# RWKV's modulation slots: none in its end, twelve in its preparation, and another order there

## The chip, the cores and the metric

The kernel runs on one core of a Trainium2 chip. The metric is device time in microseconds, the median of the runs shown. TensorE multiplies, VectorE, ScalarE and GpSimd work elementwise, and SyncE asks for the transfers of weights; the five run side by side and meet at semaphores. A stage of the kernel ends for all engines together.

## What is computed

Two blocks of a network on 256 latent and 256 context tokens of width 1024, in float32. The first block has two layers, and each is steered by a modulation, computed from the condition vectors `c` and `c_ctx`:

```python
m_l = (jax.nn.silu(c) @ mod_w + mod_b)[:, None, :]
m_c = jax.nn.silu(c_ctx) @ mod_w + mod_b
sh1_l, sc1_l, g1_l, sh2_l, sc2_l, g2_l = jnp.split(m_l, 6, axis=-1)
...
def _ada(x, g, shift, scale):
    return rmsnorm(x, g) * (1.0 + scale) + shift
```

`mod_w` is 1024 x 6144 in each layer, so both are 48 MB to be read for two rows of output. The mixer of layer 0 is half attention, half an RWKV scan over the tokens, forwards and backwards. Ahead of the scan stands this preparation:

```python
a = jax.nn.sigmoid(a0 + ad @ a2)
tw = jnp.tanh(wd)
wl = -jax.nn.softplus(-(w0 + tw @ w2)) - 0.5      # decay: exp(-exp(wl))
kk = hd(k * k_k)
kk = kk / jnp.maximum(jnp.sqrt(jnp.sum(kk * kk, axis=-1, keepdims=True)), 1e-12)
k = k * (1.0 + (a - 1.0) * k_a)
g = jax.nn.sigmoid(gd) @ g2
```

## The kernel before

The program is one stage after the other, called from `program` in the order of the network. Feature rows lie on the 128 partitions, the 512 tokens along the free dimension; a width of 512 is four tiles, `t` = 0 to 3. All weights come through `RING`, four places of 1 MB.

**Modulation slots.** The 48 MB of `mod_w` are cut into 48 slots of 1 MB, 256 columns each (class `Modulation`, L402). Slot n uses ring place n mod 4. Stages that leave ring and engines some room host a range of slots, in order. A slot is four steps: SyncE's `fetch` (L429); TensorE's `add` (L434), 8 matmuls into one half of PSUM bank 7, once the slot before it is folded; ScalarE's `copy` (L447) of the sums to SBUF, which waits for the sums and for the fold before; and TensorE's `fold` (L453), two narrow matmuls that turn the copy into columns of the other half of bank 7. There is one place for the sums and one for their copy, so slots can't overlap: the sums of a slot come after the fold of the one before. At the end of the stage VectorE's `bias` (L460) adds `mod_b` to all columns of the stage's range. The first stage hosts slots 0 to 7, the attention 8 to 29, its norm 30, then RWKV's preparation 31 to 38, its back-decay stage 39 to 43, its end 44 to 47. The chunk stages between them host none: their matrices lie in the ring. The last gains (`gain`, L470) are computed in RWKV's end, and the first MLP uses them.

**The preparation** (`rwkv_prepare_stage`, L2682). On TensorE: *rates* are the products `ad @ a2`, on array rows 64 to 127, *decays* the products `tanh(wd) @ w2_f`, on rows 0 to 63; both take 512 tokens per tile. The order is rates 0 to 2, decays 0 to 2, rate 3, decay 3; then the four norm sums (L2734, `kk * kk` over a head), each once its square and a rate's sigmoid are done, since they share PSUM banks; then sixteen transposes of v (L2743); then all eight slots. On ScalarE: Tanh, four squares, the gate's Sigmoid, then sigmoids of rates (L2760) and decays (L2762) in turn; `inverse_roots` (L2528) with a load of the table for logarithm and exponential, four logarithms, which wait for VectorE's floors of the norms, and four exponentials; three exponentials of 2048 columns (L2768 to L2771) and two short ones; then four times a slot's copy and a copy of transposed tokens (L2637), and then the four copies that are left. On VectorE: sixteen scans of the decays (L2655), four floors (L2799), the centring of the decays (L2665 to L2678), then kk and the factors with GpSimd's products between them, four products of 2048 columns, and `bias`. On SyncE: the fetches of slots 35 to 38, each when the slot four before it is summed.

**RWKV's end** (`rwkv_finish_stage`, L3117). It normalizes y and gates it; VectorE's last step is the gated product of tile 3 (L3203). SyncE fetches slots 44 to 47 at the start, and then the four parts of the output weights, each when its place's slot is summed. TensorE's slots follow its last gate product; the bias and three gains come last on VectorE. The stage behind it is the first MLP (`first_mlp_stage`, L642): ScalarE copies a rounded half of a weight tile (L522), VectorE subtracts it from the whole (L529), TensorE multiplies.

Of the kernel before, what the change touches and what calls it, by code (L numbers as in the profile page):

```python
# [30 lines left out]
ACT = mybir.ActivationFunctionType  # L31
# [9 lines left out]
NCH = TOK // CH  # L41
HID = 4096
FF = 2816
SLOTS = 4
# [2637 lines left out]
def rwkv_prepare_stage(net, mod, first_slot, last_slot):  # L2682


    nc, mem = net.nc, RwkvMemory(net)
# [6 lines left out]
    with Stage(net, "rwkv_prepare") as st:  # L2692
# [16 lines left out]
        def _(pe):  # L2709
# [10 lines left out]
            rates(0)  # L2720
            rates(1)
            rates(2)
            pe.wait_ge(tanh_ready, 1)
            for t in range(3):
                decays(t)
            rates(3)
            decays(3)
            for t in range(4):
                pe.wait_ge(squared, t + 1)
                if t < 3:  # L2730
                    pe.wait_ge(a_ready, t + 2)
                else:
                    pe.wait_ge(gated, 3)
                nc.tensor.matmul(norm_in[t], net.const(C_BLK), square[:, t, :], start=True, stop=True).then_inc(normed, 1)  # L2734
            for c in range(NCH):
                if c < 2:
                    pe.wait_ge(gated, c + 1)
                elif c == 2:
                    pe.wait_ge(gated, 4)
                else:  # L2740
                    pe.wait_ge(floor_ready, 1)
                for t in range(4):
                    last = nc.tensor.transpose(turned_in[c][:, P * t:P * t + P], mem.v_pairs[:, t, c, :],  # L2743
                                               net.const(C_IDENT))
                last.then_inc(turned, 1)
            for n in range(first_slot, last_slot + 1):
                mod.add(pe, n, first_slot)
# [3 lines left out]
        def _(act):  # L2751
            link = Chain(act, act_own)
            net.log_exp_loaded = False
            act.activation(net.PT[0:64, lora, :], net.PT[0:64, lora, :], ACT.Tanh).then_inc(tanh_ready, 1)
            for t in range(4):
                act.activation(square[:, t, :], k[t], ACT.Square, scale=net.par("l0_k_k", t)).then_inc(squared, 1)
            act.activation(net.PT[:, gate, :], net.PT[:, gate, :], ACT.Sigmoid)
            for t in range(4):
                act.wait_ge(a_summed, t + 1)
                act.activation(b[t], a_in[t], ACT.Sigmoid, bias=net.par("l0_a0", t)).then_inc(a_ready, 1)  # L2760
                act.wait_ge(summed, t + 1)
                act.activation(rows(mem.sig[:, t]), decay_in[t], ACT.Sigmoid,  # L2762
                               bias=net.par("l0_w0_f", t)).then_inc(gated, 1)
            inverse_roots(net, act, link, root_ready, [(floor_ready, t + 1, norm[:, t, :], norm[:, t, :], 1.0, 0.0)
                                                       for t in range(4)])
            kr = mem.kr.rearrange("p t c n m -> p (t c) n m")
            act.wait_ge(cum_ready, 1)
# [7 lines left out]
            for c in range(NCH):  # L2775
                mod.copy(act, first_slot + c)
                act.wait_ge(turned, c + 1)
                copy_tokens(act, mem.vtok, net.ps[(4, 5, 0, 2)[c]], c)
            for n in range(first_slot + NCH, last_slot + 1):
                mod.copy(act, n)  # L2780
# [335 lines left out]

def rwkv_finish_stage(net, mod, first_slot, last_slot, following):  # L3117

# [8 lines left out]
    with Stage(net, "rwkv_finish") as st:  # L3127
# [7 lines left out]
        @st.sync  # L3135
        def _(sp):
            for n in range(first_slot, last_slot + 1):
                mod.fetch(sp, n)
            taken = [n % SLOTS for n in range(first_slot, last_slot + 1)]
            for s in sorted(range(following.first()), key=lambda s: s in taken):  # L3140
                if s in taken:
                    sp.wait_ge(mod.summed, first_slot + taken.index(s) + 1)
                net.fetch(sp, following, 0, s)
# [7 lines left out]
        def _(pe):  # L3151
# [10 lines left out]
            for t in range(4):  # L3162
                pe.wait_ge(root_ready, t + 1)
                nc.tensor.matmul(gate[t], net.G2[:, P * t:P * t + P], net.PT[:, 25, :], start=True,
                                 stop=True).then_inc(gate_ready, 1)
            for n in range(first_slot, last_slot + 1):
                mod.add(pe, n, first_slot)
            mod.fold(pe, last_slot, first_slot)

        @st.scalar  # L3170
        def _(act):
# [4 lines left out]
            for t in range(4):  # L3176
# [3 lines left out]
                                                       for t in range(4)])  # L3180
            for n in range(first_slot, last_slot + 1):
                mod.copy(act, n)

        @st.vector
        def _(dve):
# [9 lines left out]
            for t in range(4):  # L3195
# [7 lines left out]
                nc.vector.tensor_tensor(y[:, t, :], y[:, t, :], gate[t], ALU.mult)  # L3203
            link(mod.bias(dve, (first_slot, last_slot), first_slot, last_slot))
            for layer, half_of in ((0, 1), (1, 0), (1, 1)):
# [641 lines left out]
def program(nc, ins, out):  # L3847
    with ExitStack() as ctx:
# [25 lines left out]
                                            for h, o in enumerate(heads)], TOK, 1e-5, mod=mod, slot=30)  # L3874
        rwkv_prepare_stage(net, mod, 31, 38)
        rwkv_chunks_stage(net, 0)
        rwkv_back_decay_stage(net, mod, 39, 43)
        rwkv_chunks_stage(net, 1)
        rwkv_finish_stage(net, mod, 44, 47, w_out[0])
        mod.spent(mod.FIRST, mod.ALL - 1)  # L3880
# [25 lines left out]
```

## Time and profile before

| | us |
|---|---|
| median of 3 runs | 2114.11 |
| lowest, highest | 2112.74, 2120.26 |
| profiled execution, device time | 2122.14 |
| its span | 2120.3 |
| preparation, 304.1 to 353.0 | 48.9 |
| RWKV's end, 611.4 to 635.8 | 24.4 |

The profile shows one execution. Times in its rows count from the start of the span. A row of a timeline has the start, the time from the first start to the last end, the engine, the line, the tiles written and read, the count, and, in brackets, how long the engine was idle before and what released it. A float32 matmul is two instructions (a wide and a narrow one of 16 per slot in a slot's sums). PE is TensorE, DVE VectorE, ACT ScalarE; the granted clock is given in parts of 2.4 GHz, so 0.50 is 1.2 GHz.

### The profile page before, as it was taken

To read this page: it belongs to the slowest core of one execution; us is meant where nothing else is said; L and a number is where in the kernel's file an instruction comes from. 1 tells how busy PE (TensorE), PEld (TensorE's weight loads), DVE (VectorE), ACT (ScalarE), POOL (GpSimd) and SP (SyncE) were. 2 spreads that over 40 slices of the span, in tenths; PEclk is the share of its full clock that TensorE was granted. 3 is DMA by queue.
4 is the path that set the end of the run, shared out by engine and by line. 5 is a ranking of instruction groups with operands and counts; after the bars stand their busy time and mean duration, and the time that the engine had idled before them with its cause. 6 is when DMAs were issued, how large, how long until landed. Compare 5 with 4: busy or idle time off the path is not lost. (4 is left out here: it accounts for less than half of the span.)

```text
span 2120.3 us, 41961 instructions
## 1 busy us (share of the span) xinstructions
PE 1929.4 (91%) x18072; PEld 1674.4 (79%) x18072; DVE 1203.5 (57%) x2057; ACT 838.2 (40%) x1532; POOL 295.7 (14%) x351
## 2 busy tenths in 40 slices
PE   5998887778789999999999879999989998989997
PEld 3886545767757888888978779999769998869997
DVE  3322757455445742453465858856567756577753
ACT  3321564324223421222344545544464445365432
POOL 2000304402304000002200420112021001121001
PEclk8999886997999999999999999999999999999998
DMA  9232762011042322332231055554325545324543
GB/s 323 85 100 74 255 207 81 4 48 56 4 135 85 100 97 82 100 100 92 88 119 40 21 166 162 192 181 158 100 80 166 192 152 186 100 76 154 190 154 105
DMA packets 249004, 255.04 MB, mean 120 GB/s; under 512 B 6914, under 2 KB 247187, under 8 KB 248691
## 3 DMA queue, kind: packets, MB, share of 16 engines
q1 hardware_dynamic: 247344, 251.19, 36.8%
q8 instruction: 143, 2.34, 0.5%
q0 software_dynamic: 864, 0.98, 0.2%
q14 instruction: 43, 0.34, 0.1%
q10 hardware_dynamic: 610, 0.18, 0.0%
HBM read 251.28 MB, written 1.05 MB: 119 GB/s over the span
## 5 line engine op out<-in xcount | busy, mean ns | idle before, releaser
L529 DVE TENSOR_TENSOR RING_rounded<-RING,SC_rounded 128x1024 fp32r<-128x1024 f32 (+2 forms) x390 | 459.7, 1222 | 281.9 <-ACT SC_rounded L522 281.7
L549 PE MATMUL bank<-OT_rounded,SC_rounded 128*128 128x256 f32 (+1 forms) x1808 | 576.2, 319 | 27.3 <-DVE PT L1268 11.5
L550 PE MATMUL bank<-HT_rounded,SC_rounded 128*128 128x256 f32 (+1 forms) x1808 | 572.3, 317 | 0.0
L551 PE MATMUL bank<-OT_rounded,RING_rounded 128*128 128x256 f32 (+1 forms) x1808 | 570.4, 315 | 0.0
L522 ACT ACTIVATE SC_rounded<-RING 128x1024 fp32r<-128x1024 f32 (+2 forms) x390 | 372.4, 1006 | 324.4 <-DMA RING<-in_l_mlp_w 186.2
L549 PEld LDWEIGHTS bank<-OT_rounded,SC_rounded 128*128 128x128 f32 x1808 | 345.0, 191 | 56.5 <-issue 13.6
L551 PEld LDWEIGHTS bank<-OT_rounded,RING_rounded 128*128 128x128 f32 x1808 | 344.2, 190 | 25.7
L550 PEld LDWEIGHTS bank<-HT_rounded,SC_rounded 128*128 128x128 f32 x1808 | 344.6, 191 | 22.6
L549 PE MATMUL bank<-PT_rounded,SC_rounded 128*128 128x256 f32 (+1 forms) x896 | 278.5, 311 | 4.7 <-DVE RING_rounded L529 4.7
L550 PE MATMUL bank<-PT_rounded,SC_rounded 128*128 128x256 f32 (+1 forms) x896 | 277.7, 310 | 0.0
L551 PE MATMUL bank<-PT_rounded,RING_rounded 128*128 128x256 f32 (+1 forms) x896 | 276.7, 309 | 0.0
L549 PEld LDWEIGHTS bank<-PT_rounded,SC_rounded 128*128 128x128 f32 x896 | 169.1, 189 | 16.3 <-DVE RING_rounded L529 5.7
L551 PEld LDWEIGHTS bank<-PT_rounded,RING_rounded 128*128 128x128 f32 x896 | 169.2, 189 | 10.8
L550 PEld LDWEIGHTS bank<-PT_rounded,SC_rounded 128*128 128x128 f32 x896 | 169.2, 189 | 9.5
L550 PE MATMUL bank<-OT_rounded,SC_rounded 128*128 128x256 f32 (+1 forms) x336 | 102.5, 305 | 0.0
L549 PE MATMUL bank<-HT_rounded,SC_rounded 128*128 128x256 f32 (+1 forms) x272 | 85.6, 315 | 16.2 <-DVE OT_rounded L1456 7.5
L3090 DVE TENSOR_TENSOR SC<-SC,bank 128x512 f32<-128x512 f32 (+1 forms) x80 | 51.3, 684 | 71.3 <-PE bank L2984 70.8
L795 DVE SCALAR_TENSOR_TENSOR XT<-bank,MOD,XT 128x256 f32<-128x256 f32 x48 | 21.4, 480 | 116.7 <-PE bank L551 116.7
L551 PE MATMUL bank<-HT_rounded,RING_rounded 128*128 128x256 f32 (+1 forms) x272 | 84.5, 311 | 0.0
L549 PEld LDWEIGHTS bank<-HT_rounded,SC_rounded 128*128 128x128 f32 x272 | 54.0, 198 | 19.9 <-DVE RING_rounded L529 13.0
L443 PE MATMUL bank<-RING,SC 128*32 128x256 f32 x768 | 66.2, 474 | 3.7 <-DMA RING<-in_l_mod_w 3.7
L456 PEld LDWEIGHTS bank<-CONST,SC 128*128 128x128 f32 x192 | 32.3, 238 | 46.1 <-ACT SC L451 45.0
(536 smaller groups left out, 2793.1 us busy)
## 6 DMA issues: line engine op xcount, KB each, us to landing
RING<-in_l_mlp_w SPq DMA_DIRECT2D x64, 1024.0 KB, 5.2
RING<-in_l_mod_w SPq DMA_DIRECT2D x48, 1024.0 KB, 6.9
RING<-in_w_ffn_in SPq DMA_DIRECT2D x44, 1024.0 KB, 5.1
RING<-in_l_w_in SPq DMA_DIRECT2D x25, 1024.0 KB, 5.3
RING<-in_w_ffn_out SPq DMA_DIRECT2D x16, 768.0 KB, 4.3
RING<-in_w_in SPq DMA_DIRECT2D x10, 1024.0 KB, 5.2
RING<-in_w_ffn_out SPq DMA_DIRECT2D x16, 640.0 KB, 3.9
RING<-in_l_w_out SPq DMA_DIRECT2D x8, 1024.0 KB, 6.2
```

The costliest lines, as they stand in the source:

```text
L443: last = self.nc.tensor.matmul(self.sums[group, :], self.c[:, kt, :], self.net.RING[:, s, SW * kt:SW * kt + SW], start=(i == 0), stop=(i = ...
L456: last = self.nc.tensor.matmul(self.columns[:, 2 * (n - first) + m, :], self.rows[:, P * m:P * m + P], self.net.const(C_FOLD, 2), start=Tr ...
L522: act.activation(net.high4(s, m)[:, 0:self.w.kts[s], :], net.ring_half(net.RING, s, m, self.w.kts[s]), ACT.Copy).then_inc(self.high_ready, 1)
L529: net.nc.vector.tensor_tensor(low, whole, net.high4(s, m)[:, 0:self.w.kts[s], :].bitcast(F32), ALU.subtract).then_inc(self.split_ready, 1)
L549: net.nc.tensor.matmul(bank[:, tokens], high, x_high, start=start, stop=False)
L550: net.nc.tensor.matmul(bank[:, tokens], high, x_low, start=False, stop=False)
L551: return net.nc.tensor.matmul(bank[:, tokens], low, x_high, start=False, stop=stop)
L795: return nc.vector.scalar_tensor_tensor(into, bank[:, tokens], net.MOD[:, gate + tile, j:j + 1], into, ALU.mult, ALU.add)
L3090: nc.vector.tensor_tensor(inv, inv, bank, ALU.subtract).then_inc(doubled, 1)
```

## The change

- RWKV's end hosts no slots. Its fetches, sums, copies, folds and `bias` go; the loads of the output weights wait for nothing; the three gains stay.
- The preparation hosts slots 31 to 42, twelve instead of eight. The back-decay stage hosts 43 to 47, five as before, in the same ring places.
- In the preparation TensorE does rate 0, all four decays, then rates 1 to 3, then the norms. The sums of the first two slots stand between the norms and the transposes, the others behind the transposes.
- On ScalarE the squares and the decays' sigmoids come in pairs (two squares, two sigmoids, two squares, two sigmoids), then the rates' sigmoids, then the gate's. The copies of the first two slots stand ahead of `inverse_roots`, the third behind it, and from the fourth on one stands behind each copy of tokens.

```diff
-            rates(1)
-            rates(2)
             pe.wait_ge(tanh_ready, 1)
-            for t in range(3):
+            for t in range(4):
                 decays(t)
-            rates(3)
-            decays(3)
+            for t in range(1, 4):
+                rates(t)
...
+            for n in range(first_slot, first_slot + 2):
+                mod.add(pe, n, first_slot)
             for c in range(NCH):
...
-            for n in range(first_slot, last_slot + 1):
+            for n in range(first_slot + 2, last_slot + 1):
                 mod.add(pe, n, first_slot)
             mod.fold(pe, last_slot, first_slot)
...
-            for t in range(4):
-                act.activation(square[:, t, :], k[t], ACT.Square, scale=net.par("l0_k_k", t)).then_inc(squared, 1)
-            act.activation(net.PT[:, gate, :], net.PT[:, gate, :], ACT.Sigmoid)
+            squares(range(2))
+            gates(range(2))
+            squares(range(2, 4))
+            gates(range(2, 4))
             for t in range(4):
                 act.wait_ge(a_summed, t + 1)
                 act.activation(b[t], a_in[t], ACT.Sigmoid, bias=net.par("l0_a0", t)).then_inc(a_ready, 1)
-                act.wait_ge(summed, t + 1)
-                act.activation(rows(mem.sig[:, t]), decay_in[t], ACT.Sigmoid,
-                               bias=net.par("l0_w0_f", t)).then_inc(gated, 1)
+            act.activation(net.PT[:, gate, :], net.PT[:, gate, :], ACT.Sigmoid)
+            for n in range(first_slot, first_slot + 2):
+                mod.copy(act, n)
             inverse_roots(net, act, link, root_ready, [(floor_ready, t + 1, norm[:, t, :], norm[:, t, :], 1.0, 0.0)
                                                        for t in range(4)])
+            mod.copy(act, first_slot + 2)
...
             for c in range(NCH):
-                mod.copy(act, first_slot + c)
                 act.wait_ge(turned, c + 1)
                 copy_tokens(act, mem.vtok, net.ps[(4, 5, 0, 2)[c]], c)
-            for n in range(first_slot + NCH, last_slot + 1):
+                mod.copy(act, first_slot + 3 + c)
+            for n in range(first_slot + 3 + NCH, last_slot + 1):
                 mod.copy(act, n)
...
-        rwkv_prepare_stage(net, mod, 31, 38)
+        rwkv_prepare_stage(net, mod, 31, 42)
         rwkv_chunks_stage(net, 0)
-        rwkv_back_decay_stage(net, mod, 39, 43)
+        rwkv_back_decay_stage(net, mod, 43, 47)
         rwkv_chunks_stage(net, 1)
-        rwkv_finish_stage(net, mod, 44, 47, w_out[0])
+        rwkv_finish_stage(net, mod, w_out[0])
```

`squares(some)` is the line of the squares for these tiles, and `gates(some)` waits for the decay product of each tile and takes its sigmoid. In RWKV's end the lines with `first_slot` and `last_slot` are gone, and SyncE's part is a loop of `net.fetch(sp, following, 0, s)` over the four places.

## Rows read from the trace of the kernel before

**Rows 1.** The head of the profile's page.
```profile
span 2120.3 us, 41961 instructions
```

**Rows 2.** Busy time by stretch; the line of columns stands first.
```profile
core 0: us, PE busy (x) PEld busy (x) DVE busy (x) ACT busy (x) POOL busy (x), PEclk, DMA share, GB/s
304.10:353.00 48.90, 37.48 (x200) 19.41 (x200) 34.64 (x42) 30.94 (x54) 15.82 (x8) 0.61 0.29 93
...
611.40:635.80 24.40, 21.70 (x112) 10.18 (x112) 14.45 (x24) 11.00 (x20) 4.97 (x4) 0.93 0.89 286
```

**Rows 3.** Timeline, ScalarE, the preparation: start, duration, instruction, idle before.
```profile
305.90 2.54 ACT L2756 ACTIVATE HT<-PT,PAR 128x512 f32<-128x512 f32 x4
308.46 1.28 ACT L2757 ACT_TABLE_LOAD   x1
...
315.03 1.28 ACT L2524 ACT_TABLE_LOAD   x1
317.49 2.42 ACT L2534 ACTIVATE OT<-OT 128x512 f32<-128x512 f32 x4 [1.18 <-DVE OT L2799]
...
322.05 1.90 ACT L2768 ACTIVATE PT<-SC 128x2048 f32<-128x2048 f32 x1
...
327.66 0.36 ACT L451 ACTIVATE SC<-bank 128x256 f32<-128x256 f32 x1
327.92 1.54 ACT L2637 ACTIVATE SC<-bank 64x256 f32<-64x256 f32 x4
...
351.30 0.38 ACT L451 ACTIVATE SC<-bank 128x256 f32<-128x256 f32 x1 [3.00 <-PE bank L443]
```

**Rows 4.** Timeline, TensorE, the preparation.
```profile
307.07 1.06 PE L2717 MATMUL bank<-PT,LORA 64*128 64x512 f32 x1
307.23 1.06 PE L2713 MATMUL bank<-PT,LORA 64*128 64x512 f32 x1
307.92 1.06 PE L2717 MATMUL bank<-PT,LORA 64*128 64x512 f32 x1
...
312.19 1.06 PE L2717 MATMUL bank<-PT,LORA 64*128 64x512 f32 x1
313.17 4.49 PE L2734 MATMUL bank<-HT,CONST 128*128 128x512 f32 x8
...
319.34 1.07 PE L443 MATMUL bank<-RING,SC 128*32 128x256 f32 x16
328.08 1.01 PE L456 MATMUL bank<-CONST,SC 128*128 128x2 f32 x4 [7.67 <-ACT SC L451]
```

**Rows 5.** Timeline, VectorE, the preparation.
```profile
324.67 0.74 DVE L2803 SCALAR_TENSOR_TENSOR HT<-PT,PAR,OT 128x512 f32<-128x512 f32 x1
...
352.79 0.19 DVE L466 TENSOR_TENSOR MOD<-bank,PAR 128x32 f32<-128x32 f32 x1 [6.41 <-PE bank L456]
```

**Rows 6.** Stretches, TensorE alone, then all engines: granted clock, DMA share, GB/s.
```profile
314.00:315.00 1.00, 1.00 (x3) 0.60 0.00 0
332.00:353.00 21.00, 17.76 (x123) 0.50 0.47 151
353.00:358.00 5.00, 4.64 (x44) 0.50 0.00 2
...
475.00:480.00 5.00, 3.62 (x28) 1.93 (x32) 4.86 (x8) 1.48 (x2) 0.00 (x0) 0.52 1.10 348
```

**Rows 7.** Timelines, RWKV's end: TensorE, then VectorE, then ScalarE.
```profile
625.62 1.07 PE L443 MATMUL bank<-RING,SC 128*32 128x256 f32 x16
...
627.73 1.07 PE L443 MATMUL bank<-RING,SC 128*32 128x256 f32 x16
...
630.72 0.69 DVE L3203 TENSOR_TENSOR OT<-OT,bank 128x512 f32<-128x512 f32 x1
...
635.40 0.35 DVE L473 SCALAR_TENSOR_TENSOR AFF<-MOD,PAR 128x16 f32<-128x16 f32 x3
...
636.09 2.00 ACT L522 ACTIVATE SC_rounded<-RING 128x1024 fp32r<-128x1024 f32 x2 [2.00 <-PEq L193]
```

More of the change, by code:

```diff
@@ L2754, in _, with squares, gates @@
             act.activation(net.PT[0:64, lora, :], net.PT[0:64, lora, :], ACT.Tanh).then_inc(tanh_ready, 1)
-            for t in range(4):
-                act.activation(square[:, t, :], k[t], ACT.Square, scale=net.par("l0_k_k", t)).then_inc(squared, 1)
-            act.activation(net.PT[:, gate, :], net.PT[:, gate, :], ACT.Sigmoid)
+            def squares(some):
+                for t in some:
+                    act.activation(square[:, t, :], k[t], ACT.Square, scale=net.par("l0_k_k", t)).then_inc(squared, 1)
+            def gates(some):
+                for t in some:
+                    act.wait_ge(summed, t + 1)
+                    act.activation(rows(mem.sig[:, t]), decay_in[t], ACT.Sigmoid,
+                                   bias=net.par("l0_w0_f", t)).then_inc(gated, 1)
+            squares(range(2))
+            gates(range(2))
+            squares(range(2, 4))
+            gates(range(2, 4))
             for t in range(4):
@@ L3114, in _, with rwkv_finish_stage @@
                     nc.vector.tensor_tensor(out, out, bank, ALU.add).then_inc(out_taken, 1)
-def rwkv_finish_stage(net, mod, first_slot, last_slot, following):
+def rwkv_finish_stage(net, mod, following):
     nc, eps = net.nc, 64e-5
@@ L3136, in _ @@
         def _(sp):
[L3137 to L3142, printed above, removed]
+            for s in range(following.first()):
                 net.fetch(sp, following, 0, s)
@@ L3165, in _ @@
                                  stop=True).then_inc(gate_ready, 1)
-            for n in range(first_slot, last_slot + 1):
-                mod.add(pe, n, first_slot)
-            mod.fold(pe, last_slot, first_slot)
         @st.scalar
@@ L3180, in _ @@
                                                        for t in range(4)])
-            for n in range(first_slot, last_slot + 1):
-                mod.copy(act, n)
         @st.vector
@@ L3203, in _ @@
                 nc.vector.tensor_tensor(y[:, t, :], y[:, t, :], gate[t], ALU.mult)
-            link(mod.bias(dve, (first_slot, last_slot), first_slot, last_slot))
             for layer, half_of in ((0, 1), (1, 0), (1, 1)):
```

## The prediction

> **What bounds the kernel now.** I read the page's head first: one core, a profiled span of 2120.3 us [rows 1]. Shares over the span say little about this change, so the next view is the table by stretch [rows 2]: the preparation takes 48.9 us at a mean granted clock of 0.61, RWKV's end 24.4 us at 0.93. The chunk stages between them and all that follows from 636.09 on the change does not touch; they can only start earlier or later. So the question is where each of the two stages ends. The reader should look at the last instruction of each engine in each.
>
> In the preparation ScalarE runs without a pause until 315, waits for VectorE's floors, does logarithms and roots from 317.49 on, from 322.05 three exponentials, and only then, at 327.66, the copy of the first hosted slot [rows 3]. TensorE had finished that slot's sums at 319.34 + 1.07 = 320.4 and stood idle for 7.7 us [rows 4]. From there the eight slots go one behind the other, copy to copy (351.30 - 327.66) / 7 = 3.38 us [rows 3], at a granted clock of 0.50, the 1.2 GHz level [rows 6]. VectorE's own work is over at 346.4, 6.4 us before its bias at 352.79, which waits for the last fold and ends the stage [rows 5]. **The preparation is bound by a serial line of slots behind ScalarE's roots and exponentials.**
>
> In RWKV's end a slot takes 2.11 us (627.73 - 625.62), since the clock is still high, and most of the line lies beside VectorE's gating, which ends at 631.41; the bias and the gains end at 635.75 [rows 7]. The first MLP's first weight copy follows at 636.09 [rows 7].
>
> **RWKV's end, without its four slots.** The bias goes, the three gains of 0.35 us together stay and can follow the gating: 631.41 + 0.35 = 631.76 against 635.75 [rows 7]. The gain is **4.0 us**, not four slots' time, because the rest was hidden. The four loads of the output weights are now asked for at the stage's start, behind no wait; the weight copy came straight after the stage change before, so they save nothing more and cost nothing (at worst 0, at best 0.3 us). TensorE ended cold before and will be idle a little longer; its cold start in the MLP is there in both.
>
> **Back-decay.** Its five slots are renumbered by four and keep their ring places. Zero.
>
> **The preparation, first part: TensorE.** A decay or a rate is two instructions of 0.85 us each at this clock (307.92 - 307.07) [rows 4]. In the kernel before, rates on rows 64 to 127 lie beside decays on rows 0 to 63: one starts at 307.23 between two decays at 307.07 and 307.92 [rows 4]. The new order puts all four decays in a row, then three rates in a row. Decays start at 306.05 after the Tanh and end at about 308.1, 309.8, 311.5 and 313.2, as late as before (the last decay instruction started at 312.19 [rows 4]). The first rate can overlap the last decay, the others can't: they end near 314.1, 315.8 and 317.5. So the first norm matmul starts at about 317.4 where it started at 313.17: **+4.2 us**.
>
> The Trainium skill, "TensorE: Matmul & The Clock Gate", section on packing small matmuls by row and column tiling, says that matmuls in different row groups run side by side while those of one group don't. The rows agree, and it speaks against this change: by a chip that paid nothing for the new order the +4.2 would be 0 and the sum 7.4; by the rule and the rows it is 11.6.
>
> The eight norm instructions took 4.49 us before [rows 4], the first ones at 0.85 and, after the clock had risen to 2.4 GHz, 1.6 us after the first norm had started (the mean grant of 314 to 315 is 0.60 [rows 6]), at 0.43. I found no row in which rates or decays alone brought the clock up, so I don't count on it before the norms. If all eight are warm they take 3.4, if all are cold 6.8; the chunks' start took over 4.6 us to warm [rows 6], the norms before 1.6, so I take five cold, 5.5, ending at **322.9** (320.9 to 324.3) where it was 317.7.
>
> **ScalarE and VectorE up to there.** Squares 0 and 1 end at 307.2, the Sigmoid table's load (1.28 us [rows 3]) at 308.5. Decay sigmoids at 0.57 us apart then wait for the decays: they end at 309.1, 310.6, 312.4 and 314.0 against 315.0 [rows 3]. So "decays first" brings the scans about 1.4 us forward, but VectorE then waits for the norms, and its gain is nothing. The rate sigmoids come at 313.9, 314.5, 315.9 and 317.6, the gate's ends at 318.8. Squares ran under Tanh's set before, between its load and Sigmoid's [rows 3]; that they also run under Sigmoid's is not shown; if not, two more loads of 1.28 come.
>
> **Two slots ahead of the roots.** The first slot's sums need the norms out of the way: 322.9 + 1.07 [rows 4] = 324.1, copy 0.36, fold and second sums to 326.2, second copy ends at 326.6, by the 2.11 us warm period of [rows 7]. ScalarE waits for both; queued behind these waits are its roots and exponentials, and behind the roots VectorE's kk chain and GpSimd's eight products. The load of the logarithm's table, hidden at 315.03 in a wait before, now stands in the open: 326.6 + 1.28 = 327.9. The logarithms started at 317.49 before [rows 3]: **+10.4 us**. All behind it on ScalarE moves with it, and the third slot's copy adds 0.36: exponentials at 332.8 against 322.05. VectorE's chain from kk, which started at 324.67 and ended at 346.4 [rows 5], starts with the first root at about 331.0 and ends near 352.7. That is not the bound.
>
> The Trainium skill, "ScalarE: Activation LUTs", section "What ACT_TABLE_LOAD costs", counts 1.38 us of drain beside each load's 1.28. The rows don't: a Sigmoid follows the load that started at 308.46 within 1.3 us [rows 3]. With the drain the sum would be 1.4 higher.
>
> **The tail.** From the exponentials' start to the first copy behind them were 327.66 - 322.05 = 5.6 us [rows 3]; then comes one block of token copies of 1.5 us [rows 3], now ahead of the slot's copy: the fourth slot is copied at 332.8 + 5.6 + 1.5 = 339.9. TensorE idles until then (its sums are done by 336), so it's cold, as it was at 327.66. Nine slots remain, eight periods of 3.38: the last copy at 367.0 where it was at 351.30, **+15.7 us**. SyncE's loads for slots five to twelve wait for the sums four slots back; the first two come at about 324 and 326, and loads don't bind: one slot in 3.38 us is less than the 348 GB/s that the queue gave elsewhere, 3.0 us a slot [rows 6]. What follows the last copy is the same.
>
> **Sum.** 10.4 (roots late) + 0.36 (third copy) + 1.5 (tokens first) + 3.38 (one more slot behind) = 15.6; less 4.0 = **+11.6 us**. On the profiled execution's own 2122.14 us (span 2120.3) that is 2133.8. The median shown is 2114.11, 8 us lower for the same program, so I carry the difference over: **2125.7 us**.
>
> **Rivals.**
> *The clock stays high in the tail.* If the spread slots keep TensorE warm, the period isn't 3.38 but 2.11 [rows 7], then bounded by loads at 3.0 us a slot for the last four, which are asked for only when a ring place is free (first at about 341.5): the last slot lands near 356, the stage ends near 358.5, +5.6, and the net is +1.5: 2115.6, not slower. It decides at the fourth slot: warm or cold when the line starts. For it: RWKV's end ran its first slots warm [rows 7], at a mean grant of 0.93 [rows 2]. Against: there they followed 14 us of dense work; and in 332 to 353 the same pattern never rose from 0.50 [rows 6].
> *The front part isn't the bound either.* Rates and decays overlap all the same or the clock rises early, so that the norms end at 317, the roots start at 322, and the tail is warm too: the last slot is bound by loads, near 352. Net about -5: 2109. Against it are the row pairs in [rows 4] and the two waits on ScalarE.
> *The reloads.* Square isn't in the Sigmoid set: two loads of 1.28 before the last decay sigmoids, the rate sigmoids and norms behind them, about +2.5: 2128.2. For it: nothing shows squares under this set. Against: they ran under Tanh's without a load of their own [rows 3].
> *The change does not do what it says:* if the three early copies were all that mattered (as much work hidden as moved), the tail would be 9 slots against 8, +3.4, and the net -0.6. This is the whole idea of the spread; it fails where ScalarE waits for TensorE ahead of the roots. Price 2113.5.
>
> **Chances.** Main case 0.78, with its own range of 2120 to 2131 (norms warm or cold 2 to 3 us, clock phases at the starts of chunks and MLP 1 to 2 us each, medians 1 to 2 us). Warm tail 0.08, spread as meant 0.04, front not bound 0.03, reloads 0.07. The range 2114 to 2132 takes in the warm tail and the reloads. What a measurement of this kernel can tell from no change is about 0.5%, 10.6 us; the forecast lies one us beyond it. Of the main case a good half is above: 0.78 x 0.58 + 0.07 x 0.9 = 0.52 slower; 0.03 faster; 0.45 within.
>
> **What would show it.** Right: the first norm matmul near 317.4; logarithms near 328; a gap on ScalarE between the gate's sigmoid and the first slot copy; fourth slot's copy near 340 and 3.38 us from copy to copy behind it; the bias near 368.5; RWKV's end 4 us shorter. Wrong: logarithms before 323 (the waits were hidden), copies 2.1 to 3.0 us apart (warm tail), extra table loads between squares and sigmoids, or VectorE's last product later than the last fold.

## The result and the profile after

The changed kernel takes 2126.59 us (median of 11 runs, 2120.08 to 2129.83), the kernel before 2116.55 us over the 11 runs beside them (2109.49 to 2120.44). The ratio is 1.0042, with a 95% interval from 1.0029 to 1.0056, which is +8.9 us (6 to 12). The forecast was +11.6 us.

Stages read off both traces, in us. The preparation is counted from ScalarE's first table load to the end of VectorE's `bias`, RWKV's end from TensorE's first matmul to the end of the last gain (the times are rounded after the differences are taken):

| stage | before | after | difference |
|---|---|---|---|
| ahead of the preparation | 304.1 | 303.4 | -0.6 |
| preparation | 48.9 | 61.6 | +12.7 |
| chunks, first | 115.9 | 115.4 | -0.5 |
| back-decay | 25.4 | 26.3 | +0.9 |
| chunks, second | 117.1 | 116.9 | -0.3 |
| RWKV's end | 24.3 | 20.2 | -4.1 |
| the rest | 1484.6 | 1481.4 | -3.2 |
| span | 2120.3 | 2125.2 | +4.9 |

The preparation and RWKV's end together give +8.6 us, +9.5 with back-decay; both lie in the interval of the timed runs. The span alone would say +4.9; the rest moved by 3 us in a part that nothing touched, so the spans of one pair of profiles don't settle a difference of this size. The changed stages can be compared one by one.

The stretches that answer to [rows 2] (columns as there):

```profile
303.40:365.10 61.70, 47.08 (x280) 24.15 (x280) 35.23 (x42) 32.56 (x58) 15.86 (x8) 0.62 0.44 142
623.60:643.90 20.30, 14.22 (x32) 5.91 (x32) 14.20 (x23) 9.46 (x16) 4.98 (x4) 0.96 0.64 207
```

TensorE's timeline of the preparation, to set beside [rows 4] (L2717 are decays, L2713 rates):

```profile
309.01 1.22 PE L2713 MATMUL bank<-PT,LORA 64*128 64x512 f32 x1
309.85 1.06 PE L2717 MATMUL bank<-PT,LORA 64*128 64x512 f32 x1
310.02 1.06 PE L2713 MATMUL bank<-PT,LORA 64*128 64x512 f32 x1
...
311.41 0.59 PE L2713 MATMUL bank<-PT,LORA 64*128 64x512 f32 x1
313.27 1.12 PE L2713 MATMUL bank<-PT,LORA 64*128 64x512 f32 x2 [1.27 <-ACT PT L2772]
314.32 5.40 PE L2732 MATMUL bank<-HT,CONST 128*128 128x512 f32 x8
319.65 1.07 PE L443 MATMUL bank<-RING,SC 128*32 128x256 f32 x16
...
329.32 1.02 PE L456 MATMUL bank<-CONST,SC 128*128 128x2 f32 x4 [3.25 <-ACT SC L451]
330.27 1.93 PE L443 MATMUL bank<-RING,SC 128*32 128x256 f32 x16
336.77 1.01 PE L456 MATMUL bank<-CONST,SC 128*128 128x2 f32 x4 [4.57 <-ACT SC L451]
```

The rates 1 and 2, issued behind all decays, run beside the last two decays: they start at 309.01, 310.02, 310.87 and 311.41 and end at 312.0. Then TensorE waits 1.27 us for ScalarE before rate 3, and the norms follow rate 3. The first norm stands 10.9 us behind the stage's start where it stood 9.1 behind it. The eight norm instructions take 5.40 us where they took 4.49. A slot's sums take 1.07 us at first and 1.93 once TensorE has waited 3.25 us for ScalarE's third copy.

ScalarE's timeline, to set beside [rows 3]:

```profile
315.01 0.62 ACT L2773 ACTIVATE PT<-PT 128x512 f32<-128x512 f32 x1
320.79 0.38 ACT L451 ACTIVATE SC<-bank 128x256 f32<-128x256 f32 x1 [5.15 <-PE bank L443]
322.90 0.38 ACT L451 ACTIVATE SC<-bank 128x256 f32<-128x256 f32 x1 [1.73 <-PE bank L443]
323.30 1.28 ACT L2524 ACT_TABLE_LOAD   x1
324.59 2.19 ACT L2534 ACTIVATE OT<-OT 128x512 f32<-128x512 f32 x4
...
336.33 0.38 ACT L451 ACTIVATE SC<-bank 128x256 f32<-128x256 f32 x1
...
363.38 0.38 ACT L451 ACTIVATE SC<-bank 128x256 f32<-128x256 f32 x1 [3.00 <-PE bank L443]
```

Here is the change in seven lines: ScalarE waits 5.15 and 1.73 us for the first two slots, the table's load stands behind them in the open, the logarithms come 21.1 us into the stage instead of 13.4, and from the fourth copy on the line runs at (363.38 - 336.33) / 8 = 3.38 us. VectorE had its products done at 349.2 and waits; the line that answers to [rows 5]:

```profile
364.86 0.21 DVE L466 TENSOR_TENSOR MOD<-bank,PAR 128x48 f32<-128x48 f32 x1 [15.64 <-PE bank L456]
```

RWKV's end on VectorE, to set beside [rows 7]: the gains follow the last gated product directly.

```profile
642.89 0.69 DVE L3206 TENSOR_TENSOR OT<-OT,bank 128x512 f32<-128x512 f32 x1
643.50 0.34 DVE L473 SCALAR_TENSOR_TENSOR AFF<-MOD,PAR 128x16 f32<-128x16 f32 x3
```

### The profile page after: what moved, and what is told of

It is laid out like the page before. It is cut to its first block and busy times, and to the rows that moved or that the text cites. A ratio compares the mean times of both kernels' runs of the same rounds, so it can differ in the third digit from the quotient of the medians.

```text
span 2125.2 us, 41960 instructions
## 1 busy us (share of the span) xinstructions
PE 1927.4 (91%) x18072; PEld 1670.5 (79%) x18072; DVE 1201.6 (57%) x2056; ACT 838.3 (39%) x1532; POOL 296.1 (14%) x351
## 5 line engine op out<-in xcount | busy, mean ns | idle before, releaser
L549 PEld LDWEIGHTS bank<-OT_rounded,SC_rounded 128*128 128x128 f32 x1808 | 345.1, 191 | 56.7 <-issue 13.5
L775 ACT ACTIVATE PT<-bank 128x512 f32<-128x512 f32 x32 | 18.9, 598 | 123.9 <-PE bank L551 123.9
```

The lines of the kernel that those rows point to most:

```text
L549: net.nc.tensor.matmul(bank[:, tokens], high, x_high, start=start, stop=False)
L775: act.activation(hidden.whole[:, 2 * q + m, :], part.bank(q, m)[:, :], ACT.Relu).then_inc(part.taken, 1)
```

## Experiments

The theory to test: the preparation ends with a serial line of slots, whose period is set by TensorE's clock, and RWKV's end gives back only what was not hidden. All runs are timed beside the kernel before, 5 to 12 times each; the ratio of a run is its time over that of the kernel before, with its 95% interval behind it. "Into the stage" counts from ScalarE's first table load of the preparation. *Warm* is a granted clock of 1.00 (2.4 GHz), *cold* one of 0.50 (1.2 GHz), and the *period* is the time from one slot's copy to the next. Stage times come from one profiled execution of each run.

### The two halves of the change, each alone

The allotment of the change with the old order of the preparation:

```diff
-        rwkv_prepare_stage(net, mod, 31, 38)
+        rwkv_prepare_stage(net, mod, 31, 42)
...
-        rwkv_finish_stage(net, mod, 44, 47, w_out[0])
+        rwkv_finish_stage(net, mod, w_out[0])
```

> The allotment of the change alone (31 to 42 in the preparation, none in RWKV's end) with the preparation's order of the kernel before. Theory (the preparation ends with the serial line of slots, 3.38 us each behind ScalarE's exponentials): first copy 24 us after the stage's first ScalarE instruction as before, eleven periods of 3.38 behind it, so the preparation is 4 x 3.38 = 13.5 us longer than before, RWKV's end 4.0 shorter, net +9.5 us, ratio 1.0045. That is about what the whole change measured, so its new order is worth nearly nothing. Rival (the new order is what costs): without it the time stays within 0.15% of before. Rival (the new order saves much): over +13 us.

The ratio is 1.0043 (1.0026 to 1.0059). The first copy comes 23.6 us into the stage and the twelfth at 60.75; the stage takes 62.45 us and RWKV's end 20.2. That is as the theory has it.

The new order with the old allotment (the change's `rwkv_prepare_stage`, the rest of the kernel before):

> The change's new order in the preparation alone, with the allotment of before (31 to 38, 39 to 43, 44 to 47). Theory: the fourth copy comes 32.9 us after the stage's first ScalarE instruction, as in the changed kernel, and four periods of 3.38 follow it instead of nine slots' eight: the preparation is 61.6 - 13.5 = 48.1 us against 48.9; VectorE's products then end near its line of slots, 46 us after the start, so they do not bind. Net -0.8 us, ratio 0.9996. Rival (the order itself costs some 9 us): ratio above 1.003.

The ratio is 0.9997 (0.9983 to 1.0012) and the stage takes 48.06 us, as expected; the last copy is at 46.4 us and VectorE's products end at 45.8. So **the +0.42% is the allotment's, and the order is worth nothing that can be measured.** Its three early copies shorten the line by three periods, 10 us, and its late logarithms (+7.7), plus a block of token copies now ahead of the fourth copy (+1.5), give nearly all of that back.

RWKV's end alone. This kernel leaves out the fetches, sums, copies and folds of slots 44 to 47 and sets their columns, the last gate, to zero, so what it computes is not the network:

```diff
-            link(mod.bias(dve, (first_slot, last_slot), first_slot, last_slot))
+            nc.vector.memset(net.MOD[:, 88:96, :], 0.0).then_inc(own, 1)
+            dve.wait_ge(own, link.n + 1)
```

> The kernel before with slots 44 to 47 left out altogether (the last eight columns of the modulation are set to zero), so RWKV's end is that of the changed kernel and nothing else is moved. Theory: most of the four slots was hidden beside VectorE's gating, so the end is 4.0 us shorter and the kernel too, ratio 0.9981. Rival (the slots cost their full 4 x 2.11 = 8.4 us, or free loads start the MLP earlier): ratio 0.996.

The ratio is 0.9957 (0.9942 to 0.9972). The trace shows that stage at 20.35 us, 3.9 shorter, and a span 3.2 us shorter; the timed runs show 9 us (6 to 12). The stage is as the theory has it, but the timed kernel gained more than its stage, which is the number of the rival, and this stays open. The profiled execution was the slowest of the five, 2118.98 us where the median is 2111.75. In it no stage holds 8 us, and the MLP's first weight copy starts 0.3 us behind the gains, as in the kernel before, so the rival's reasons don't show either. The run with the allotment alone has the same empty end, and there the stages (+13.5 and -4.1) account for the whole. What the zeros do to the time behind this stage was not tested.

### What delays the logarithms

The table's load moved ahead of the two copies, in the changed kernel:

```diff
+            load_log_exp(net, act)
             for n in range(first_slot, first_slot + 2):
                 mod.copy(act, n)
```

> The changed kernel with the load of the table for logarithm and exponential placed ahead of the first two slot copies, where ScalarE waits for TensorE anyway. Theory: the logarithms start 1.28 us earlier and all behind them, the line of slots too: the preparation 60.3 us instead of 61.6, ratio to before 1.0036 where the change has 1.0042. Rival (copies need another table, or the load is followed by a drain): no gain, or a second load in the trace.

The ratio is 1.0047 (1.0034 to 1.0060), so there is no gain, and the stage takes 62.6 us. ScalarE's timeline of this run, and TensorE's rate 3:

```profile
308.84 1.28 ACT L2524 ACT_TABLE_LOAD   x1
314.73 0.38 ACT L451 ACTIVATE SC<-bank 128x256 f32<-128x256 f32 x1 [4.61 <-PE bank L443]
316.84 0.38 ACT L451 ACTIVATE SC<-bank 128x256 f32<-128x256 f32 x1 [1.73 <-PE bank L443]
317.12 2.18 ACT L2534 ACTIVATE OT<-OT 128x512 f32<-128x512 f32 x4
```

```profile
305.52 2.07 PE L2713 MATMUL bank<-PT,LORA 64*128 64x512 f32 x2 [1.19 <-ACT PT L2772]
```

The load is hidden now: from the second copy to the logarithms it's 0.28 us instead of 1.69. But in this execution TensorE's eight norm instructions took 6.14 us instead of 5.40 and started 12.5 us into the stage instead of 10.9, at the lower clock, so the first sums came 2.4 us later and ate the 1.4. The edit isn't the cause of that: the load stands behind the sigmoids that the norms need, and the run with filler in the changed kernel, without this edit, also has its first norm at 12.5. The load is hidden as expected; that the stage gets shorter by it is not shown, and 1.3 us is less than the timed runs can tell.

Rates 1 and 2 ahead of the decays again, in the changed kernel:

```diff
             rates(0)
+            rates(1)
+            rates(2)
             pe.wait_ge(tanh_ready, 1)
             for t in range(4):
                 decays(t)
-            for t in range(1, 4):
-                rates(t)
+            rates(3)
```

> The changed kernel with rates 1 and 2 issued ahead of the decays again, so that both row groups of the array are in use together; decays 0 to 3 still ahead of rate 3. Theory (rates behind decays delay the norms): rates 1 and 2 are done 3 us earlier, but in the changed kernel TensorE stood idle 1.27 us before rate 3 for the first rate's sigmoid, which itself comes behind the decays' sigmoids on ScalarE, so the first norm moves at most 1 us forward; what may change more is the clock at the norms, granted 0.50 in the changed kernel (5.40 us for eight) and 1.00 at best (3.4 us). The stage is 0 to 3 us shorter. Rival (the issue order is what delays the norms, +4.2 us as predicted): the logarithms start over 3.5 us earlier.

The ratio is 1.0049 (1.0032 to 1.0066), and the stage takes 61.97 us. TensorE's timeline of this run:

```profile
299.62 1.06 PE L2713 MATMUL bank<-PT,LORA 64*128 64x512 f32 x1
300.19 1.06 PE L2717 MATMUL bank<-PT,LORA 64*128 64x512 f32 x1
300.47 1.06 PE L2713 MATMUL bank<-PT,LORA 64*128 64x512 f32 x1
301.04 3.14 PE L2717 MATMUL bank<-PT,LORA 64*128 64x512 f32 x6
306.19 2.07 PE L2713 MATMUL bank<-PT,LORA 64*128 64x512 f32 x2 [2.01 <-ACT PT L2773]
308.19 5.61 PE L2733 MATMUL bank<-HT,CONST 128*128 128x512 f32 x8
```

Rates 1 and 2 are done early, and TensorE only waits longer ahead of rate 3, 2.01 us for the first rate's sigmoid. The first norm starts 11.0 us into the stage, the changed kernel's 10.9, but the two are alike by two differences that cancel: the clock was up during the decays and down again behind them (1.00 in 302 to 305, 0.50 in 305.5 to 308), so rate 3 starts at 9.0 us instead of 9.8 and takes 2.07 us instead of 1.12. What tells is the wait. In the changed kernel too, rates 1 and 2 are over with the decays and rate 3 waits 1.27 us, and 1.19 in the run with the table's load ahead of the copies, which is cold up to the norms. **What delays the norms is ScalarE's order (all decay sigmoids ahead of the first rate's, whose bank rate 3 needs), not TensorE's.** No run puts the first rate's sigmoid back ahead of the decays' alone.

### What sets the period

The kernel before, with matmuls that nobody reads behind each slot's sums, so that TensorE doesn't rest:

```diff
+            def filler(count, width):
+                for _ in range(count):
+                    nc.tensor.matmul(net.ps[3][:, 0:width], net.const(C_ONES), net.CONST[:, 0:width], start=True, stop=True)
+
+            pe.wait_ge(floor_ready, 4)
             for n in range(first_slot, last_slot + 1):
                 mod.add(pe, n, first_slot)
+                filler(*((8, 512) if n == first_slot else (1, 256)))
```

The filler writes to a bank from which VectorE takes the last floors' input, hence the wait for them; the first sums start about 15.2 us into the stage, as before.

> The kernel before with products nobody reads on TensorE: eight of 512 columns behind the first slot's sums, while ScalarE is busy, and one of 256 columns behind each later slot's sums. Theory (the period of 3.38 us is that of TensorE at the lower clock): the clock stays high in the line of slots, the period falls to between 2.2 and 3.0 us (the loads' bound at 348 GB/s for 1 MB), the line ends at 24 + 7 x 2.2 to 3.0 = 39 to 45, and the stage at 44 to 46 us instead of 48.9; net -3 to -5 us, ratio 0.998. Rival (the period is set by the chain of semaphores and copies whatever the clock): period over 3.2 us, and the filler adds to it.

The ratio is 0.9970 (0.9957 to 0.9983), and the stage takes 42.45 us. The granted clock (TensorE alone, columns as in [rows 6]) and three of the copies:

```profile
319.00:327.00 8.00, 7.63 (x28) 1.00 0.41 133
327.00:343.00 16.00, 15.12 (x156) 1.00 0.61 198
```

```profile
328.94 0.38 ACT L451 ACTIVATE SC<-bank 128x256 f32<-128x256 f32 x1 [0.29 <-PE bank L443]
...
331.05 0.38 ACT L451 ACTIVATE SC<-bank 128x256 f32<-128x256 f32 x1 [0.30 <-PE bank L443]
...
333.17 0.38 ACT L451 ACTIVATE SC<-bank 128x256 f32<-128x256 f32 x1 [0.29 <-PE bank L443]
```

The clock stays at 2.4 GHz and the period is 2.11 us, with a matmul more in it than the 3.38 us one; only the last copy comes 2.8 us behind the one before it, since its load is late. The line now ends beside VectorE's products, which end the stage. So the period is set by TensorE's clock.

The changed kernel with the same, three and six wide ones behind the third and fourth slot's sums and one narrow one behind each later slot's:

> The changed kernel with products nobody reads behind the sums of slots three to twelve, three and six of 512 columns where ScalarE is busy, one of 256 columns behind each later slot. Theory (the change is slow only since its slots run at the lower clock, as the filler run on the kernel before showed for its own): fourth copy at 32.9 us after the stage's start as in the changed kernel, then a period of 2.11, or up to 3.0 where the loads bind, since eight slots are now asked for one by one: last copy at 50 to 57, the preparation 51 to 58 us instead of 61.6, ratio to before 0.998 to 1.001. Rival (the loads bind harder, as ring places come free late): period over 3.0 and the stage over 59 us.

The ratio is 1.0006 (0.9989 to 1.0023), and the stage takes 55.07 us. The fourth copy is 35.3 us into the stage (the norms were late and cold in this execution, the first at 12.5), then six copies follow 2.11 to 2.19 us apart and the last two 2.98 and 2.76. This is the warm tail that the prediction had as a rival, with a net of +1.5 us; +1.3 (-2.3 to +4.9) is measured, which agrees within a wide interval.

### Copies where ScalarE doesn't wait

The kernel before with its first copies ahead of each long exponential and behind the last:

```diff
+            mod.copy(act, first_slot)
             act.activation(kr[:, :, 1, :], flat(mem.cum), ACT.Exp, scale=-DECAY).then_inc(exped, 1)
+            mod.copy(act, first_slot + 1)
             act.activation(flat(mem.bd), flat(mem.cum), ACT.Exp, scale=DECAY).then_inc(exped, 1)
+            mod.copy(act, first_slot + 2)
             act.wait_ge(cum_ready, 2)
...
+            mod.copy(act, first_slot + 3)
             for c in range(NCH):
-                mod.copy(act, first_slot + c)
                 act.wait_ge(turned, c + 1)
                 copy_tokens(act, mem.vtok, net.ps[(4, 5, 0, 2)[c]], c)
+                mod.copy(act, first_slot + 4 + c)
```

> The kernel before, its order and its allotment, with the first four slot copies placed where ScalarE never waits for them: ahead of each of the three long exponentials and behind the last. Theory: each costs ScalarE 0.3 us and takes a period of 3.38 off the line behind it; copies 2 to 4 may follow each other at ScalarE's 2.1 us, so four slots are done by about 25 us after the stage's start and four are left: the line ends at about 24.9 + 4 x 3.38 = 38.5, which puts VectorE's products at the end, 42.3 + 1: the stage 43.5 to 44 us instead of 48.9. Net -5, ratio 0.9976. Rival (the copies delay the exponentials and these VectorE's products as much as they save): within 1 us of before.

The ratio is 0.9972 (0.9958 to 0.9986), and the stage takes 43.28 us. The sum came out as forecast, by another way: the copies were 3.4 us apart from the first on, not 2.1, since TensorE had rested 2.8 us ahead of the first copy.

```profile
320.89 0.36 ACT L451 ACTIVATE SC<-bank 128x256 f32<-128x256 f32 x1
321.15 1.90 ACT L2769 ACTIVATE PT<-SC 128x2048 f32<-128x2048 f32 x1
324.24 0.38 ACT L451 ACTIVATE SC<-bank 128x256 f32<-128x256 f32 x1 [1.20 <-PE bank L443]
...
327.62 0.38 ACT L451 ACTIVATE SC<-bank 128x256 f32<-128x256 f32 x1 [1.19 <-PE bank L443]
```

It brings the line 5.6 us forward, since the first copy comes at 18.0 instead of 23.6 us into the stage, and it costs VectorE nothing: its products end at 42.3 as before.

One slot more here and one less in RWKV's end (31 to 39, 40 to 44, 45 to 47):

> As the run with the copies among the exponentials, but nine slots in the preparation, five in back-decay and three in RWKV's end. Theory: the line of nine ends 3.4 us later, at about 42, still beside VectorE's products, so the preparation stays at 44; RWKV's end loses its one slot behind VectorE's gating, 2.7 us (the fourth slot was run at the lower clock). Net -7.5 us, ratio 0.9965. Rival (no slot is free any more): the preparation is 3.4 us longer than in the run with eight and the net no better.

The ratio is 0.9961 (0.9942 to 0.9980). The preparation takes 46.68 us, 3.4 longer than with eight slots in the run above, which is the rival's; RWKV's end takes 21.15, where the run above has 23.3. The two ratios can't be told apart. At the lower clock there's no free slot.

### Both together, and where the slots belong

Copies among the exponentials, filler in the preparation (three wide ones behind the first slot's sums, one narrow behind each later slot's) and, with four wide ones ahead of its first slot and five behind its second, in back-decay; three allotments.

> The order of the kernel before, twelve slots in the preparation and none in RWKV's end as in the change, the first four copies among the exponentials, filler in the preparation's and in back-decay's line of slots. Theory: copies from 18.0 us on at 2.11, then at the loads' 3.0 us a slot; slot five is asked for at 15.2 us, so the twelfth lands at about 15 + 5 + 7 x 3.0 = 41 to 42 and the line ends at 44, level with VectorE's products: preparation 44 to 46 us (48.9 before), RWKV's end 20.2 (24.3), back-decay 23 (25.4). Net -9 to -11 us, ratio 0.995 to 0.996. Rival (loads bind, each asked for only when a place is free): preparation over 48, net less than -6.

The ratio is 0.9953 (0.9936 to 0.9969). The preparation takes 47.27 us, back-decay 25.18 and RWKV's end 20.21. The twelfth copy comes 46.0 us into the stage: from the eighth slot on, TensorE waits for loads.

```profile
327.52 1.07 PE L443 MATMUL bank<-RING,SC 128*32 128x256 f32 x16 [0.71 <-DMA RING<-in_l_mod_w]
...
330.50 1.07 PE L443 MATMUL bank<-RING,SC 128*32 128x256 f32 x16 [0.79 <-DMA RING<-in_l_mod_w]
...
333.64 1.07 PE L443 MATMUL bank<-RING,SC 128*32 128x256 f32 x16 [0.96 <-DMA RING<-in_l_mod_w]
```

3.0 to 3.1 us a slot, as estimated from [rows 6], but the twelfth slot's sums start 44.8 us into the stage, where its landing was put at 41 to 42. In back-decay the filler didn't keep the clock up in this execution: the granted clock is 0.51 in 459 to 466.

> The same with the allotment of before (8, 5, 4): copies among the exponentials, filler in preparation and back-decay. Theory: the preparation is bound by VectorE, 42.5 us; back-decay 23; RWKV's end 24.3: net -8.5 us, ratio 0.996; the four slots taken out of RWKV's end in the run with twelve would then be worth 4.0 less what the preparation is longer. Rival (filler costs power and the clock falls elsewhere, or the rest of the kernel is slower): stages as told but the whole not.

The ratio is 0.9956 (0.9939 to 0.9973). The preparation takes 42.45 us and is ended by VectorE, back-decay takes 22.85, at a granted clock of 1.00, and RWKV's end 24.34. Timed, twelve and eight slots come out level. By the stages twelve cost 4.8 us in the preparation and give 4.1 in RWKV's end; the 2.3 us between the two back-decay stages is their clock.

> Copies among the exponentials and filler in preparation and back-decay, with ten slots in the preparation, five in back-decay, two in RWKV's end. Theory: in the run with twelve the tenth copy came 40.2 us after the stage's start, so ten slots end at 41.7, beside VectorE's work, which ends at 42.4: preparation 42.5 to 43; two slots in RWKV's end take 4.2 us behind the gate products and end beside VectorE's gating, so that stage is 20.3 to 20.6. Against before -6 (preparation), -2.4 (back-decay), -3.8 (RWKV's end): -12 us, ratio 0.9943. Rival (RWKV's end still shows a slot): that stage 22 us, and the ratio that of the runs with eight or twelve, 0.9955.

It takes 2101.29 us (median of six) against 2118.66, a ratio of **0.9917** (0.9897 to 0.9937), the fastest version of all. The preparation takes 42.47 us, back-decay 22.85 and RWKV's end 20.41. The last rows of both stages on VectorE show that neither has a wait in front of `bias`:

```profile
335.41 2.29 DVE L2826 TENSOR_TENSOR PT<-PT 128x2048 f32<-128x2048 f32 x1
337.62 0.19 DVE L466 TENSOR_TENSOR MOD<-bank,PAR 128x40 f32<-128x40 f32 x1
```

```profile
609.92 0.69 DVE L3220 TENSOR_TENSOR OT<-OT,bank 128x512 f32<-128x512 f32 x1
610.52 0.16 DVE L466 TENSOR_TENSOR MOD<-bank,PAR 128x8 f32<-128x8 f32 x1
610.72 0.35 DVE L473 SCALAR_TENSOR_TENSOR AFF<-MOD,PAR 128x16 f32<-128x16 f32 x3
```

The stages account for 6.4 + 2.6 + 3.9 = 12.9 us of the 17.6 (13 to 22). The other 4.7 are, as in the run with the empty end, not found in a stage that was changed. In the profile the two chunk stages are 1.8 and 1.3 us shorter than in the kernel before, but over all profiles these stages, which no run touches, take 113.7 to 118.8 and 115.9 to 120.8 us, so one profile doesn't show where the rest was gained.

## Why the prediction was right

**What bounds the stage** held: a serial line behind ScalarE's exponentials, at 3.38 us a slot at 1.2 GHz. The filler runs show the clock as its cause, and the run with the allotment alone shows the price, four periods.

**RWKV's end**: forecast -4.0, measured -4.1, by the step that was given (the gains directly behind the gating). The size belongs to this execution of the kernel before, whose fourth slot ran partly cold (0.59 granted in 631.5 to 635.7). In the runs with the order alone and with the copies among the exponentials the same four slots ran warm and the stage took 23.3 us, which would make the gain 3.1.

**Back-decay**: forecast 0, measured +0.9 in this profile. The run with the order alone has 25.40, the one with filler in the preparation alone 26.32. In the changed kernel this stage's eight decay instructions took 5.93 us instead of 3.67, at a mean grant of 0.61 instead of 1.00, since the clock fell 1.3 us into the stage. In the filler run it fell there too; in every run without filler in this stage in which it stayed high for 2.5 us or more the stage takes 25.4 whatever the preparation hosts, twelve slots included. So the +0.9 is the clock's in this execution, not the new numbering's.

**TensorE's first part** is the step that failed. It put the first norm 4.2 us later; it came 1.8 us later. The sentence that fails is "The first rate can overlap the last decay, the others can't". In the changed kernel rates 1 and 2 lie beside the last two decays and end at 312.0 with them, where the prediction had them end at about 314.1 and 315.8, and rate 3, the only one left over, waits for the first rate's sigmoid. So a delay is there, but by ScalarE's order and not by rates standing in a row. The prediction computed when that sigmoid would come, but by its row of rates it wouldn't have been waited for. In the two executions of this order that stay cold the first norm comes at 12.5 us, 3.4 later than before; that leaves 0.8 of the 2.4 us of error to this step.

The other 1.6 us are the clock. "I found no row in which rates or decays alone brought the clock up" was taken for a reason. In the changed kernel it did rise during the decays, at about 311, fell again at about 314.5, under the norms, and came back at about 318:

```profile
306.00:312.00 6.00, 6.00 (x12) 0.58 0.00 0
314.00:315.00 1.00, 1.00 (x2) 0.74 0.00 0
315.00:317.00 2.00, 2.00 (x4) 0.50 0.00 0
318.00:320.00 2.00, 2.00 (x12) 1.00 0.00 0
```

The run with the order alone has the same rise; the two cold ones don't, so it is not a property of the kernel. The old order shows it as well: in six of its nine profiles the clock is up about 4 us into the stage and the first norm comes at 8.2 us, in three, the kernel before among them, at 9.1. The logarithms start at 13.4 in all nine. Before, the norms had room; in the new order they have none.

The Trainium skill's rule on row groups ("TensorE: Matmul & The Clock Gate", section on packing small matmuls) agrees with the overlap in both traces. Rates and decays lie in different row groups in either order; the prediction took the order of issue to end their overlap, and it did not.

**The norms**: 5.5 forecast, 5.40 measured, cold for the first 3.4 us and then warm. That it fits so well is partly luck: four of the eight were cold where five were put, and the clock had been up before the norms began. Where it hadn't, they took 6.14 us.

**Two slots ahead of the roots**: the two waits and the load in the open stood where they were forecast, 2.5 us from the first sums' end to the second copy's end (326.6 - 324.1) where 2.6 are measured (323.3 - 320.7), and 1.3 of load. The logarithms came +7.7 instead of +10.4; the difference of 2.7 is the 2.4 us of the first norm and 0.3 of the steps behind it.

**The drain** that the Trainium skill counts with a table load ("ScalarE: Activation LUTs", section "What ACT_TABLE_LOAD costs") does not show: from the load at 323.30 to the first logarithm at 324.59 are 1.29 us.

**The tail** had all its terms right, eight periods of 3.38, the tokens' 1.5 and the third copy's 0.36; the last copy came +12.7 instead of +15.7 since its start did.

**The rivals.** The warm tail's price agrees with the run with filler in the changed kernel; it didn't come by itself. The reloads didn't come: the two later squares ran under the Sigmoid set without a load. The total of +11.6 lies inside the interval of 6 to 12 us, and the chances leaned to slower by over 0.5% (0.52) rather than within (0.45); the 2.7 us by which the logarithms came earlier than forecast, 2.4 of them the first norm's, are what put them on the wrong side of that line. That the forecast time of 2125.7 us lies within 1 us of the measured 2126.59 is luck: the difference was 2.7 us too large, and the three runs on which it was put had a median 2.4 us below that of all eleven.

## What to carry to other kernels

Moving a serial chain of small steps from a stage where most of it is hidden to one where its tail is bare costs its full period, here at half the clock; count only what ends behind the other engines, on both sides. An early step on an engine saves a period only where its input is already there: copies placed among the exponentials, where little waits, made the stage 5.6 us shorter, and placed ahead of the roots nothing that could be measured. When TensorE's chain is short matmuls with waits between them, look at the granted clock first; matmuls that nobody reads took over a third off the period.

## What was not expected of the hardware

The part ahead of the preparation is the same in all fourteen kernels, yet the preparation starts at anything from 294.6 to 307.0 us. The profiles fall into two groups: in the eight that start it at 302.5 to 307.0, the kernel before and the changed one among them, the granted clock is 0.92 in 200 to 290 us; in the six that start it at 294.6 to 297.2 it is 0.95 to 0.98. TensorE alone, columns as in [rows 6]:

```profile
200.00:290.00 90.00, 72.10 (x652) 0.92 0.85 273
```

```profile
200.00:290.00 90.00, 73.53 (x678) 0.96 0.92 298
```

The first is the kernel before, the second the run with ten, five and two slots. Why an execution falls into one group or the other is not shown. This part of the span is as wide as the effect under study.
